# Attention one of a fused two-block kernel: forget term, third states and gate moved between engines, a new fill order, and modulation pieces streamed elsewhere

## What is computed

```python
mod = silu(c) @ ada_w[layer] + ada_b[layer]        # 6 sections of 1024: shifts, scales, gates
h = rms_norm(x, g) * (1 + scale) + shift            # for each sublayer
# layer 0: gated spatial mixer, SwiGLU; then keys and values for layer 1:
kvf = h @ kv_w                                      # k, v, and 16 forget logits
dcum = cumsum(log_sigmoid(f_logit + kv_b_f))        # D[t], one per head
# layer 1, attention one ("fox"), 16 heads of 64, causal:
qg = h @ b_w_qg;  q = rms_norm(q) ;  gate = sigmoid(qg[1024:])
logits = q @ k.T / 8 + D[t] - D[s]
y = (softmax(logits) @ v * gate) @ b_w_o
```

## Time and profile before

| | |
|---|---|
| median of three runs | 1772.69 us |
| profiled execution, its own time | 1772.38 us |
| its span | 1770.6 us |
| PE busy | 1721.9 us (97%) |
| DVE, ACT busy | 1149.8 us (65%), 896.5 us (51%) |
| granted TensorE clock, mean | 0.994 |
| bytes read | 360.43 MB, 204 GB/s over the span |

### The profile page before, as it was taken

One profiled execution on the slowest core, in us unless ns is written; L12 is line 12 of the kernel. 1 busy time (PEld: TensorE's weight loads), 2 busy tenths in 40 slices (PEclk: granted clock), 3 DMA queues, 4 the chain that ended last, 5 costly groups with the idle time before them and its releaser, 6 DMA issues.

```text
span 1770.6 us, 22295 instructions
## 1 busy us (share of the span) xinstructions
PE 1721.9 (97%) x9048; PEld 1435.9 (81%) x9048; DVE 1149.8 (65%) x1600; ACT 896.5 (51%) x1280; POOL 7.7 (0%) x21
## 2 busy tenths in 40 slices
PE   8999999999989999999999989999999999999998
PEld 6798788888767888888889868888888889778887
DVE  6888978789858654655557967554655456675553
ACT  4655544464666444544445476444544455574432
POOL 0000000000000000000000000000000000000000
PEclk9999999999999999999999999999999999999999
DMA  9958677856535655654554325545554565245551
GB/s 385 402 225 322 247 302 287 319 216 264 209 120 188 251 194 178 216 181 172 193 209 150 127 77 182 185 168 195 202 190 176 180 227 213 96 155 189 167 191 48
DMA packets 54840, 362.93 MB, mean 205 GB/s; under 512 B 5825, under 2 KB 9025, under 8 KB 14546
## 3 DMA queue, kind: packets, MB, share of 16 engines
q1 hardware_dynamic: 52978, 350.95, 54.0%
q0 software_dynamic: 1760, 10.56, 1.5%
HBM read 360.43 MB, written 1.05 MB: 204 GB/s over the span
## 4 chain that ended last, share of the span: by engine, by line
PE 78%; DVE 11%; ACT 3%; issue 1%; DMA 0%; ACTq 0%; DVEq 0%
PE pp L634 74%; DVE low L1930 4%; DVE raw L1943 2%; PE pp L909 2%; PE pp L841 1%; DVE hf L2074 1%; ACT wh L1386 1%; PE pp L986 1%; DVE tb L1930 0%; DVE hl L1930 0%; DVE x L1933 0%; DVE sc L2326 0%; DVE top L2323 0%; DVE h L1930 0%; DMA raw<-in_w 0%
## 5 line engine op out<-in xcount | busy, mean ns | idle before, releaser
L1930 DVE TENSOR_TENSOR low<-raw,wh 128x2048 fp32r<-128x2048 f32 (+3 forms) x346 | 638.4, 1861 | 361.2 <-ACT wh L1386 360.7
L1386 ACT ACTIVATE wh<-raw 128x2048 fp32r<-128x2048 f32 (+3 forms) x352 | 537.2, 1544 | 427.0 <-PE pp L634 290.8
L634 PE MATMUL pp<-wh,hh 128*128 128x512 f32 x1312 | 521.0, 397 | 6.9 <-ACT hh L1653 2.2
L634 PE MATMUL pp<-low,hh 128*128 128x512 f32 x1312 | 510.9, 391 | 1.9 <-DVE low L1930 1.7
L634 PE MATMUL pp<-wh,hl 128*128 128x512 f32 x1312 | 506.3, 391 | 3.5 <-DVE hl L1930 3.5
L634 PEld LDWEIGHTS pp<-wh,hh 128*128 128x128 f32 x1312 | 246.9, 188 | 64.8 <-issue 11.5
L634 PEld LDWEIGHTS pp<-wh,hl 128*128 128x128 f32 x1312 | 246.5, 188 | 57.1 <-DVE hl L1930 4.8
L634 PEld LDWEIGHTS pp<-low,hh 128*128 128x128 f32 x1312 | 247.0, 188 | 51.3 <-DVE low L1930 3.1
L634 PE MATMUL pp<-wh,hidh 128*128 128x512 f32 x592 | 232.3, 392 | 0.0
L634 PE MATMUL pp<-wh,hidl 128*128 128x512 f32 x592 | 230.8, 390 | 0.0
L634 PE MATMUL pp<-low,hidh 128*128 128x512 f32 x592 | 230.8, 390 | 0.0
(11 more groups left out here) (230 smaller groups left out, 1185.8 us busy)
## 6 DMA issues: line engine op xcount, KB each, us to landing
raw<-in_w SPq DMA_DIRECT2D x300, 1024.0 KB, 4.8
raw<-in_w SPq DMA_DIRECT2D x24, 768.0 KB, 4.3
raw<-in_w SPq DMA_DIRECT2D x13, 512.0 KB, 19.2
firstw<-in_w SPq DMA_DIRECT2D x6, 1024.0 KB, 14.8
gain<-in_w POOLq DMA_DIRECT2D x6, 512.0 KB, 4.6
bT<-in_rel POOLq DMA_DIRECT2D x1, 2048.0 KB, 11.4
cst<-in_csts POOLq DMA_DIRECT2D x1, 1029.0 KB, 10.6
xT<-in_xT SPq DMA_DIRECT2D x1, 1024.0 KB, 5.7
```

The costliest lines, as they stand in the source:

```text
L634: return e.matmul(out, lhsT, rhs, start=start, stop=stop, skip_group_check=True)
L1386: q.then_inc(e.activation(wh[j % NW][:, c], raw_of(i, kt * n)[:, c], ACT.Copy), s_wh, (j, part))
L1930: return e.tensor_tensor(out, a, b, op)
```

## The change

The modulation pieces get another pace: 24 instead of 20 of them lie between weight pieces 20 and 46 of the stream's main part, six pieces (38 to 43) that lay among q1, gate1 and o come before gate's last piece, and none is left between weight pieces 65 and 78. The forget term keeps one tile dH whose partitions 32 to 63 and 96 to 127 are overwritten by the rest, so that one product of 64 rows replaces two of 32; its one left and eight right sides are made by ACT. ACT forms h3 from the turned tokens (16 operations of 128x128). The sigmoid becomes exp(min(x,0) - ln(1+exp(-|x|))): Abs, Exp, Ln and Exp on ACT with no other table, min and subtract on DVE. The fill takes six steps in round 0 and has more empty steps.

```diff
-    marks = [(0, 0), (6, 4), (8, 4), (18, 12), (20, 12), (52, 32), (56, 32), (72, 44), (78, 44), (88, 48)]
+    marks = [(0, 0), (6, 4), (8, 4), (18, 12), (20, 12), (46, 36), (54, 36), (58, 40), (60, 40), (64, 44), (78, 44), (88, 48)]
...
         def fox_rate(i):
-            return 2 if i < 5 else 1
+            return 6 if i == 0 else 2 if i < 6 else 1
...
# PE, scores
-                            rr = slice(32 * (h % 4), 32 * (h % 4) + 32)
-                            for i in range(2):
-                                ins = mm(..., dL[i][rr, 128 * u["qb"]:128 * u["qb"] + 128],
-                                         dR[i][h // 4][rr, 0:nk], False, i == 1)
+                            rr = u["rows"]
+                            ins = mm(..., dL[rr, 128 * u["qb"]:128 * u["qb"] + 128],
+                                     dR[h // 2][rr, 0:nk], False, True)
...
# PE, fox_fill
+                q.wait_ge(s_sideact, ("gate_abs", 0, 1))
                 yield from group("q1", 0, h(3), (s_side, ("qk", "q1")), fillp)
                 yield
+                yield
                 head_norm("q1", t_r)
+                yield
+                yield
                 yield "second"
-                yield from group("gate1", 0, h(3), (s_gate, ("gate", 1)), fillp)
+                yield from group("gate1", 0, h(3), (s_side, ("gate_min", 1, 0)), fillp)
+                yield
                 yield "own"
+                q.wait_ge(s_sideact, ("gate_abs", 1, 1))
...
# ACT
+            def gate_abs(g, ring):
+                _, before = ta.begin(("gate", g), (s_side, ("gate_less", g)))
+                q.wait_ge(*before)
+                a = ta.of(("gate", g))[:, :, :]
                 q.wait_ge(s_mm, (("gate", "gate1")[g], 0, "end"))
-                q.then_inc(e.activation(gT[:, 4 * g:4 * g + 4, :], ring.of(...).tiles, ACT.Sigmoid), s_gate, ("gate", g))
-                log_tables()
+                for n in range(2):
+                    t = slice(2 * n, 2 * n + 2)
+                    if n:
+                        q.wait_ge(s_side, ("gate_min", g, 1))
+                    q.then_inc(e.activation(a[:, t, :], ring.of(...).tiles[:, t, :], ACT.Abs),
+                               s_sideact, ("gate_abs", g, n))
+            def gate_log(g):
+                ...
+                q.then_inc(e.activation(a, a, ACT.Exp, scale=-1.0), s_sideact, ("gate_exp", g))
+                q.wait_ge(s_sideact, ("gate_exp", g))
+                q.then_inc(e.activation(a, a, ACT.Ln, bias=1.0), s_sideact, ("gate_log", g))
+            def gate_sigmoid(g):
+                o = gT[:, 4 * g:4 * g + 4, :]
+                q.wait_ge(s_side, ("gate_less", g))
+                q.then_inc(e.activation(o, o, ACT.Exp), s_gate, ("gate", g))
...
# ACT, fox_fill
-                yield from ahead.steps("q1", 0, "T")
+                for n, _ in enumerate(ahead.steps("q1", 0, "T")):
+                    if n == 7:
+                        gate_sigmoid(0)
+                    yield
                 head_squares("q1", fillp)
                 yield
+                yield
                 head_roots("q1", t_r)
+                yield
+                yield
                 yield "second"
                 yield from ahead.steps("gate1", 0, "T")
-                gate_sigmoid(1, fillp)
+                gate_abs(1, fillp)
+                gate_log(1)
+                yield
                 waiting("fox", 4, gT)
                 yield "own"
+                gate_sigmoid(1)
...
# ACT, before attention
+            def third_h(m):
+                ...   (waits for hT(3, m, c) of PE)
+                        ins = e.activation(h3[:, m, k, :], misc.of(("hT", 3, m, c))[:, 128 * i:128 * i + 128], ACT.Identity,
+                                           bias=shift[:, k:k + 1], scale=acols[:, k:k + 1])
+            def forget_sides():
+                ...
+                e.activation(dL[:, :], dH[:, :], ACT.Identity, bias=fc[:, 1:2], scale=fc[:, 0:1])
+                for j in range(8):
+                    ins = e.activation(dR[j][:, :], dH[:, :], ACT.Identity, bias=fc[:, 10 + j:11 + j], scale=fc[:, 2 + j:3 + j])
             for g in range(2):
-                ahead.group("kv_k", g)
+                ahead.group("kv_k", g, between=lambda: third_h(g))
...
             values(("vv", 1), "kv_v", 1, vv[:, :, 512:1024])
-            ahead.group("q", 0)
+            forget_sides()
+            ahead.group("q", 0, upto=1)
             head_squares("q")
             ahead.first("gate", 0)
             head_roots("q")
-            gate_sigmoid(0, pairs)
+            gate_abs(0, pairs)
+            gate_log(0)
...
# DVE
+            def gate_min(g, ring):
+                q.wait_ge(s_mm, (("gate", "gate1")[g], 0, "end"))
+                for n in (1, 0):
+                    ...   (n == 0 waits for gate_abs(g, 0))
+                    q.then_inc(e.tensor_scalar(gT[...], ring.of(...).tiles[:, t, :], 0.0, None, ALU.min),
+                               s_side, ("gate_min", g, n))
+            def gate_less(g):
+                o = gT[:, 4 * g:4 * g + 4, :]
+                q.wait_ge(s_sideact, ("gate_log", g))
+                q.wait_ge(s_side, ("gate_min", g, 0))
+                q.then_inc(tt(o, o, ta.of(("gate", g))[:, :, :], ALU.subtract), s_side, ("gate_less", g))
...
# DVE, fox_fill
-                yield from ahead.steps("q1", 0, "T")
+                for n, _ in enumerate(ahead.steps("q1", 0, "T")):
+                    if n == 6:
+                        gate_less(0)
+                    yield
                 head_begin("q1")
+                yield
+                yield
+                yield
                 yield
                 head_scale("q1", qg, qT[:, 4:8, :], fillp)
                 yield "second"
                 yield from ahead.steps("gate1", 0, "T")
+                gate_min(1, fillp)
+                yield
+                gate_less(1)
                 for tile in range(4):
                     lo_of(4, tile, gT[:, tile, :])
                 yield "own"
...
# DVE, before attention
-            ahead.group("kv_k", 0, between=lambda: h_parts(3, 0, *inputs_of("q")))
+            ahead.group("kv_k", 0)
...
# (the same for kv_k 1)
-            q.then_inc(tt(dD[:, :], dT[:, :], dH[:, :], ALU.subtract), s_side, "dD")
-            q.wait_ge(s_side, "dD")
-            for i, d in enumerate((dH, dD)):
-                e.tensor_scalar(dL[i][:, :], d[:, :], fc[:, 0:1], fc[:, 1:2], ALU.mult, ALU.add)
-                for j in range(4):
-                    ins = e.tensor_scalar(dR[i][j][:, :], d[:, :], fc[:, 2 + j:3 + j], fc[:, 6 + j:7 + j], ALU.mult, ALU.add)
-            q.then_inc(ins, s_side, "dR")
+            for r in (slice(32, 64), slice(96, 128)):
+                q.then_inc(tt(dH[r, :], dT[r, :], dH[r, :], ALU.subtract), s_side, ("dD", r.start))
...
             head_scale("q", qg, qT[:, 0:4, :])
+            gate_min(0, pairs)
             fill = Fill(fox_fill())
```

More of the change, by code:

```diff
@@ L148 @@
 CSTS = [("ident", 128), ("bd64", 128), ("rot64", 128), ("rot32", 128), ("cos64", 256),
[L149 removed]
+        ("sin64", 256), ("cos32", 256), ("sin32", 256), ("causal", 256), ("chunk", 256), ("forget", 18), ("tri", 128)]
 CST, NCST = {}, 0
@@ L175, in constants @@
     z = np.zeros((128, 128))
-    forget = np.zeros((128, 10))
+    forget = np.zeros((128, 18))
     forget[:, 0] = p % 32 < 16
     forget[:, 1] = p % 32 >= 16
-    for j in range(4):
-        for g in range(4):
-            forget[32 * g + 16 + 4 * j + g, 2 + j] = -1.0
-            forget[32 * g + 4 * j + g, 6 + j] = 1.0
+    for j in range(8):
+        for g in range(2):
+            for part in range(2):
+                forget[64 * g + 32 * part + 16 + 2 * j + g, 2 + j] = -1.0
+                forget[64 * g + 32 * part + 2 * j + g, 10 + j] = 1.0
     made = {"ident": np.eye(128),
@@ L352, in build @@
         lf = [place(f"lf{i}", [128, T], F32, big + 34816 + 1024 * i) for i in range(3)]
[L353 to L356, removed]
+        dH = place("dH", [128, T], F32R, big + 34816)
+        dL = place("dL", [128, T], F32R, big + 33792)
+        dR = [place(f"dR{j}", [128, T], F32R, big + 36864 + 1024 * j) for j in range(8)]
         aq = place("aq", [128, 4, T], F32, big)
@@ L1201, in tensor_program @@
             whole("q", 0, h(3), (s_side, ("qk", "q")))
-            whole("gate", 0, h(3), (s_gate, ("gate", 0)), between=lambda: head_norm("q"))
+            whole("gate", 0, h(3), (s_side, ("gate_min", 0, 0)), between=lambda: head_norm("q"))
             into_attention()
@@ L2262, in lo_of @@
                 s_lo.at["h", hv, tile, 0] = s_lo.n
+            def gate_min(g, ring):
+                q.wait_ge(s_mm, (("gate", "gate1")[g], 0, "end"))
+                for n in (1, 0):
+                    t = slice(2 * n, 2 * n + 2)
+                    if n == 0:
+                        q.wait_ge(s_sideact, ("gate_abs", g, 0))
+                    q.then_inc(e.tensor_scalar(gT[:, 4 * g + 2 * n:4 * g + 2 * n + 2, :],
```

(7 more changed lines are left out.)

28 lines of the change are left out of this document (21 added, 7 removed).

## The result

The changed kernel takes **1779.65 us** (median of seven runs, 1776.29 to 1783.26) against 1772.69 (1770.54 to 1774.85) before: ratio 1.0038, 95% interval 1.0028 to 1.0048, so 5.0 to 8.5 us slower. The forecast was 1775.4 in a range of 1766 to 1782. The profiled execution is the lowest of the seven, 1776.29 us with a span of 1774.2; that is 3.9 above the profiled execution of before (3.6 by the spans). The other six have mean clocks from 0.991 down to 0.988 where they are longest.

What follows compares the result with a forecast made beforehand. PE, busy 97% of the span, was taken as the bound. Terms 2.5 + 3.6 + 0.65 - 4.2 + 0.5 = +3.0 us on 1772.4 gave 1775.4 us; range 1766 to 1782, the forecast's own 1771 to 1779.

Steps and rivals of the forecast that it cites:

- rival C: Feed-forward: load ring sets the pace, five turns each 1.4 us short, clock drop 1.6 behind turn 0; 1780.5 us, chance 0.22.
- the shift reaches the end: Behind attention: PE is the bound, so the +3.0 us carries through to the kernel's end.
- attention's term: Attention one: rounds 0 to 4, rounds 5 to 10, gate, d products, and a wait at gate_less(1); +0.5 us in all.
- Modulation pieces in the feed-forward: Feed-forward turns: +2.5 us at turn 0 from full DVE, +3.6 at later turns from loads released in pairs.
- The last turn's 0.8: Feed-forward's last turn: a released pair stands ahead of the weight and the up projection is shorter; +0.8 us.
- Between the feed-forward and q: Low part of piece 55: one modulation piece ahead of it makes PE wait; +0.65 us, bounds 0 to 1.2.
- Third states and forget term: Start of projection q: DVE is relieved, PE's gaps fall from 3.25 to 0.6 and the clock stays up; -4.2 us.
- the d products: Attention: 32 units issue one d matmul instead of two, 3.2 us less PE work, some 2.5 where PE works through.
- Rounds 0 to 4: Attention's start: six fill steps ahead of scores 1 delay turns and leave one round owed at gate1; +1.8, bounds -2 and +4.
- The gate: Ahead of projection o: ACT's new chain makes PE wait 4.5 us instead of 2.2; +2.3, bounds -2 and +4.

Runs made afterwards that it cites:

- M alone: Kernel before with only the new marks (pace of the modulation pieces): 1781.16 us, ratio 1.0040.
- P alone: Kernel before with only the forget term of 64 rows and the third states on ScalarE; old marks, fill and gate: 1764.62 us, ratio 0.9955.
- with useless products: Changed kernel plus useless rounded 128x256 products in PE's waits, 18 at turn 0 and 38 ahead of o, once: 1777.00 us, ratio 1.0021.
- M late: Kernel before with the new marks, but modulation pieces at the old pace until weight piece 24: 1777.36 us, ratio 1.0027.
- F alone: Kernel before with 64-row forget term, third states on ScalarE and the new fill order; old gate, old marks: 1771.85 us, ratio 0.9998.
- P+G: Kernel before with 64-row forget term, third states on ScalarE and the new gate; old fill, old marks: 1770.26 us, ratio 0.9989.
- F and G: New fill order and new gate; timed together in the changed kernel with the old marks: 1775.78 us, ratio 1.0017.
- P+M: Kernel before with 64-row forget term, third states on ScalarE and the new marks, without new fill or gate: not run, no time.
- fill spread: Changed kernel with fill steps of 3 in each of rounds 0 to 3, 2 in rounds 4 and 5, then 1: 1775.89 us, ratio 1.0021.
- first try of the useless products: Changed kernel plus useless products with float32 operands, 18 at turn 0 and 38 ahead of o, the 38 run again: 1810.35 us.

## Why the prediction came out as it did

The sign was right, and 1779.65 lies in the stated range, but not in the forecast's own range of 1771 to 1779: 4.2 us of the median are not in its terms. It lies close to rival C's 1780.5, and C was not right as a whole either: of its five short turns behind turn 0, two came in the changed kernel's profile.

The profiles can be compared part by part, by the starts of the same PE instructions. The borders are the turn at 174.18 us of the kernel before, the product with `hl` at 372.74, the first step of the fill at 454.73 and the product with `ones` at 526.12. Each column is the difference to the kernel before, in us; the last one is the change with useless products of the right size.

| part | forecast | change | M alone | P alone | with useless products |
|---|---|---|---|---|---|
| before 174 us | 0 | -0.9 | -0.1 | -0.9 | -0.1 |
| feed-forward 0 | +6.1 | +6.7 | +8.2 | 0.0 | +8.1 |
| up to the fill | -3.55 | -2.9 | +1.3 | -4.1 | -2.9 |
| attention | +0.5 | +3.5 | -0.2 | -2.8 | +0.1 |
| behind it | 0 | -2.8 | -2.7 | -2.1 | -2.6 |
| whole span | +3.0 | +3.6 | +6.6 | -9.9 | +2.6 |

That the profiled span is 3.6 us longer, near the forecast, is luck. At the end of attention the change is 6.4 us late. The first and the fifth row are not its work. Near 54 us DVE waits for a load (`binr`), which came about 0.9 us earlier in the profiles of the change and of P. Behind attention the forecast said that the shift reaches the end; but the kernel before had low clocks there in its one profile, in work that the change leaves alone:

```profile
1503.00:1524.00 21.00, 20.10 (x156) 17.43 (x156) 13.38 (x46) 10.35 (x36) 0.00 (x0) 0.92 0.32 112
```
```profile
1508.00:1528.00 20.00, 18.77 (x158) 16.10 (x160) 13.68 (x48) 10.84 (x38) 0.00 (x0) 1.00 0.35 129
```

(The first line is the kernel before, the second the same work in the changed one: clock 0.92 against 1.00, and 1.5 us less time.) P's span gains by it too: -9.9 in the profile, -8.0 by the runs.

**The step that failed** is attention's term, "1.8 - 1.5 + 2.3 - 2.5 = +0.1" and 0.4 more. It took its waits about as long as they came, and all work behind them at full clock, at a price of nothing. Measured, attention is 3.5 us longer, with the clock at 0.57 and 0.76 behind turn 0's and gate1's waits. With the waits at turn 0 and o filled it is +0.1, close to the forecast: the missing 3 us are the clock (3.0 by the runs, 3.4 by the two profiles).

Part by part:

- *Modulation pieces in the feed-forward:* +2.5 and +3.6 forecast. The waits at turns 0 to 2 came as worked out (5.96 us against 0.57). M late shows that turn 0 is DVE's full stretch and the others the released pairs. The last turn's 0.8 did not come. The part is 6.7 us longer and its waits 5.4; the other 1.3 is spread over the turns, at a clock of 1.00, and its cause stays open. In four other profiles with these marks, with turn 0's wait of 3.05, the clock fell right behind it (0.66 over 208 to 212 with M alone). The forecast gave this to rival C and argued it away with one wait of 2.2 us that had left the clock up; that argument was wrong.
- *Between the feed-forward and q:* 0.57 us against +0.65.
- *Third states and forget term:* -4.2 at q, and 2.5 for the d products. P alone has -4.1 up to the fill and -2.8 in attention, both as forecast; the wait at q is 0.81 us where 0.6 was expected. The rule of the Trainium skill ("ScalarE: Activation LUTs", section "Rules for kernel authors") is to use VectorE for adds and multiplies. Here 24 such passes on ScalarE cost it 9.8 us beside PE's work and the kernel became faster (0.9955), so in this place the row decided.
- *Rounds 0 to 4:* +1.8 forecast. The waits came where the lined-up programs put them (2.40 and 1.79), at half clock from 473 on.
- *The gate:* the wait of 4.5 us came as 4.74. But its cause is only in part the new chain: F alone makes 4.14 with the old sigmoid. That the size was met with the new chain alone in the sum is luck. That the four passes and their hand-over cost more than the two table loads they save is borne out by P+G (3.13 us ahead of o against 2.47 in P alone).

By the runs, F and G cost 7.6 and 6.0 us on top of P and 11.0 together (1.0017 less 0.9955). With the new marks beside them it would be 7.6 (6.7 for the change, less 7.1 for M, plus 8.0 for P), if M and P add up; P+M was not run. In all: -8.0 for P, +11.0 for F and G, +3.7 for M beside them makes the +6.7 of the ratio. The forecast had F and G at +4.5 (1.8, 2.3 and 0.4).

The profiled execution lies 3.4 us below the median. Five profiles have the new marks in full, and in feed-forward 0 it is the quickest of them. The drop behind turn 0, which it alone lacks, is worth about 1.4 us (8.1 and 8.2 against 6.7), an estimate. In the fill spread and in the first try of the useless products turn 4 waits as well, 1.60 and 2.12 us, which the forecast gave to rival C, and the part is 9.5 and 11.7 us longer:

```profile
306.21 1.23 PE L912 MATMUL pp<-cst,tb 128*128 128x128 f32 x8 [1.60 <-DVE tb L1989]
```

Which of these the other six runs had stays open, since they have no profile.

## What to carry to other kernels

When PE is 97% busy, price a new wait twice: its length, and the work behind it at half clock; take both from waits of the same length in the trace, and do not trust one wait that left the clock up. Compare two profiles part by part before you trust their spans: here the parts that nothing changed differ by 2.8 us. A change of several parts is to be timed part by part: here one part holds all of the gain, 8.0 us, and the three others cost 14.7 together.

## What the runs showed that was not expected

- The same wait may or may not bring the clock down. 3.06 us at turn 0 left it at 1.00 in the changed kernel's profile, 3.05 in M alone brought it to 0.66; 2.15 us ahead of o left it in the kernel before and not in M alone (0.57 over 516 to 524).
- Idle slots filled with rounded products of 128x256 (0.12 us each) kept it at 1.00 in attention and won 3.0 us. In P, whose waits are 1.6 and 2.5 us, they won nothing. The same with float32 operands took 0.43 us each.
- A drop of the clock delays work without making the next wait longer. At 475.67 the head sums took 3.75 us instead of 1.97, and gate1 began 7.7 us behind their start instead of 5.8 (with the useless products). But its wait is 1.79 us in both, and also with the fill spread.
